# One-hot rows of the second key: the subtraction moved from ScalarE's biased Abs to one GpSimd instruction per four tokens

## The reference

```python
def chunk(xc):
    ...
    sc = jnp.einsum('chpd,hpkd->chpk', q, sub_keys)          # two sets of 128 sub keys per head
    sv, si = lax.top_k(sc, PEER_TOPK)
    ...
    idx = jnp.take_along_axis(cidx, fi, axis=-1)             # expert = 128 * first key + second key
    g = jax.nn.softmax(fv, axis=-1)
    u = u_tab[idx]
    a = jax.nn.gelu(jnp.einsum('chkd,cd->chk', u, xc))
    vv = v_tab[idx]
    return jnp.einsum('chk,chkd->cd', g * a, vv)
```

## Time and profile before

| | us |
|---|---|
| median of 3 runs | 2059.51 |
| lowest and highest of them | 2057.79, 2061.49 |
| the profiled execution's own time | 2063.19 |
| its span from first to last instruction | 2061.5 |
| PE busy | 1805.8 (88% of the span) |
| DVE busy | 1194.0 (58%) |
| ACT busy | 908.6 (44%) |
| POOL busy | 333.3 (16%) |

### The profile page before, as it was taken

How to read it: one execution, slowest core, us unless ns; L and a number is a source line. 1 busy time by engine, 2 the same in 40 slices (tenths; PEclk the granted TensorE clock), 3 DMA queues, 4 the chain that set the end, 5 groups by cost and what they waited for, 6 DMA issues and landing times.

```text
span 2061.5 us, 36645 instructions
## 1 busy us (share of the span) xinstructions
PE 1805.8 (88%) x11980; PEld 1636.2 (79%) x11980; DVE 1194.0 (58%) x2304; ACT 908.6 (44%) x1664; POOL 333.3 (16%) x206
## 2 busy tenths in 40 slices
PE   7999799998979887977878798889998659999997
PEld 6899578787979667965878688889997558888886
DVE  2685566665444454454542699984445985555554
ACT  2564431312334444433342233335446994555553
POOL 2000000000000000020000276668884000000000
PEclk9999999999989998988898899999999999999999
DMA  8755112121436203510452254456552016666553
GB/s 280 217 183 172 32 31 61 31 61 61 141 105 183 72 0 110 181 61 0 143 130 55 84 161 151 148 152 180 180 177 71 0 45 207 192 193 192 192 192 119
DMA packets 214867, 254.91 MB, mean 124 GB/s; under 512 B 14919, under 2 KB 196907, under 8 KB 214827
## 3 DMA queue, kind: packets, MB, share of 16 engines
q1 hardware_dynamic: 214827, 254.39, 40.5%
HBM read 253.29 MB, written 1.05 MB: 123 GB/s over the span
## 4 chain that ended last, share of the span: by engine, by line
PE 55%; issue 20%; DVE 8%; POOL 7%; ACT 4%; DMA 3%; SPq 1%; DVEq 1%; POOLq 0%; ACTq 0%; PEldq 0%
PE ps L1875 17%; PE ps L1520 15%; POOL w_lo L540 6%; PE ps L1833 3%; DVE raw L1460 3%; DMA raw<-in_u_experts 3%; PE ps L1688 2%; PE ps L1648 2%; PE ps L1647 2%; PE ps L1638 2%; DVE arena L1134 2%; PE ps L1562 1%; PE ps L1621 1%; DVE raw L1341 1%; SPq L446 1%
## 5 line engine op out<-in xcount | busy, mean ns | idle before, releaser
L540 POOL TENSOR_TENSOR w_lo<-raw,w_hi 128x1024 fp32r<-128x1024 f32 x128 | 307.3, 2406 | 345.3 <-ACT w_hi L878 344.3
L1520 PE MATMUL ps<-x_hi,w_hi 128*128 128x256 f32 x1104 | 323.1, 293 | 26.7 <-DVE w_lo L950 13.9
L1833 PE MATMUL ps<-x_hi,w_hi 128*128 128x256 f32 x1024 | 297.4, 290 | 33.8 <-ACT arena L883 26.3
L1520 PE MATMUL ps<-x_lo,w_hi 128*128 128x256 f32 x1104 | 320.8, 291 | 0.0
L1520 PE MATMUL ps<-x_hi,w_lo 128*128 128x256 f32 x1104 | 320.7, 290 | 0.0
L1833 PE MATMUL ps<-x_lo,w_hi 128*128 128x256 f32 x1024 | 294.6, 288 | 0.0
L1833 PE MATMUL ps<-x_hi,w_lo 128*128 128x256 f32 x1024 | 294.3, 287 | 0.0
L1520 PEld LDWEIGHTS ps<-x_hi,w_hi 128*128 128x128 f32 x1104 | 220.6, 200 | 30.4 <-issue 14.2
L1485 DVE TENSOR_TENSOR w_lo<-raw,w_hi 128x1024 fp32r<-128x1024 f32 x128 | 156.9, 1226 | 148.3 <-ACT w_hi L938 148.3
L878 ACT ACTIVATE w_hi<-raw 128x1024 fp32r<-128x1024 f32 x128 | 135.6, 1060 | 239.6 <-DVE raw L1341 239.6
L1833 PEld LDWEIGHTS ps<-x_hi,w_hi 128*128 128x128 f32 x1024 | 201.1, 196 | 37.8 <-ACT arena L883 23.3
(11 more groups left out here) (322 smaller groups left out, 3328.8 us busy)
## 6 DMA issues: line engine op xcount, KB each, us to landing
raw<-in_u_experts SPq DMA_DIRECT2D x512, 128.0 KB, 2.6
raw<-in_v_experts SPq DMA_DIRECT2D x128, 512.0 KB, 3.5
arena<-in_ada_w SPq DMA_DIRECT2D x14, 1024.0 KB, 5.3
raw<-in_a_w_in SPq DMA_DIRECT2D x12, 1024.0 KB, 5.5
arena<-in_a_w_in SPq DMA_DIRECT2D x12, 1024.0 KB, 5.4
raw<-in_b_w_in SPq DMA_DIRECT2D x8, 1024.0 KB, 5.6
arena<-in_b_w_in SPq DMA_DIRECT2D x8, 1024.0 KB, 5.6
raw<-in_w_in SPq DMA_DIRECT2D x8, 1024.0 KB, 5.4
```

Of the source, the lines that this page charges most:

```text
L540: pool.tensor_tensor(UTL[e], UT[e % 2], UTH[e].bitcast(F32), ALU.subtract).then_inc(utl_ready, 1)
L1520: ins = mm(o[:, b * S:b * S + S], w[:, slot, kk, b * P:b * P + P], xx[:, kk, :], start=(kk == 0 and n == 0), stop=(kk == k - 1 and n == 2))
L1833: ins = mm(ps[e % 2][:, 0:S], w[e % 4][:, kk * P:kk * P + P], xx[:, kk, :], start=(kk == 0 and n == 0), stop=(kk == KC - 1 and n == 2))
```

## The change

POOL gets the subtraction: for each group it waits for the free slot (`g_ps`), then adds `iota`, read four times over, and the columns of minus b of four tokens, each read 128 times over, and writes 4 x 128 columns into the slot of `OHJ` in one `tensor_tensor`. It counts a new semaphore, `ohj_diff`. ACT waits for that instead of `g_ps` and takes Abs of all 512 columns in one activation, in place, with no bias. `rows_j` is as it was. `distance` now counts on 512 columns, one instruction in place of four. The DMA of the convolution's weights is counted by `vec_in` too, and `conv_in` is gone; PE waits for 15 DMAs on `vec_in` instead of for 14 and one.

```diff
-        x_in, conv_in, vec_in, rows_in = sem("x_in"), sem("conv_in"), sem("vec_in"), sem("rows_in")
+        x_in, vec_in, rows_in = sem("x_in"), sem("vec_in"), sem("rows_in")
+        ohj_diff = sem("ohj_diff")
...
-            sp.dma_start(S1, a_conv_w.rearrange("a i (b p) -> (a i b) p", p=P)).then_inc(conv_in, 16)
+            sp.dma_start(S1, a_conv_w.rearrange("a i (b p) -> (a i b) p", p=P)).then_inc(vec_in, 16)
...
+            pool.wait_ge(hkt_ready, 2)
+            with pool.Fori(0, S // 16) as i:
+                for c in range(4):
+                    pool.wait_ge(g_ps, 4 * i + (c + 1))
+                    tok = HKT[:, 1, bass.ds(16 * i + 4 * c, 4)].unsqueeze(2).broadcast_to([P, 4, NK])
+                    pool.tensor_tensor(OHJ[:, c, :, :], iota.unsqueeze(1).broadcast_to([P, 4, NK]), tok, ALU.add).then_inc(ohj_diff, 1)
...
             def distance(c, i):
-                g = c % 4
-                act.wait_ge(g_ps, 4 * i + (c + 1))
-                for q in range(4):
-                    ins = act.activation(OHJ[:, g, q, :], iota, ACT.Abs, bias=HKT[:, 1, bass.ds(16 * i + (4 * c + q), 1)])
-                ins.then_inc(ohj_abs, 1)
+                act.wait_ge(ohj_diff, 4 * i + (c + 1))
+                act.activation(OHJ[:, c % 4, :, :], OHJ[:, c % 4, :, :], ACT.Abs).then_inc(ohj_abs, 1)
...
-            pe.wait_ge(conv_in, 16)
-            pe.wait_ge(vec_in, 16 * 14)
+            pe.wait_ge(vec_in, 16 * 15)
```

## The result

The changed kernel takes 2087.55 us (median of 4 runs, 2084.08 to 2088.48), the kernel before 2059.74 in the 4 runs beside it. The ratio is 1.0132 (95% interval 1.0115 to 1.0150): the change costs 27.8 us. The profiled execution took 2088.19, with a span of 2086.5.

The account below looks back on a forecast made before the run. ACT was taken to bound the one-hot stage, DVE close behind; 59 turns at 2.61 us and two groups at 1.70 after the start end it 51.4 us later: 2059.5 + 51.4 = 2111 us, range 2082 to 2134.

Parts of the forecast that it names:

- ACT's relief: One-hot stage: ACT sets the pace, DVE a close second; freeing ACT wins at most 0.06 to 0.15 us per group.
- free period of 1.70: One-hot stage: DVE's time per group when it waits for nobody, 1.70 us, taken from readings of 1.72 and 1.63.
- The rival of the other sign: Line 1460 not excluded by POOL, DVE runs free: stage gains 3.7 to 8 us, 2055 us in all; chance 0.12.
- The exclusion: POOL and DVE's tensor_scalar at line 1460 wait for each other's whole instruction; one held by POOL ends 0.09 us later.
- 285 + 65 = 350 against 342: Line 1460's duration, estimated at the fast rate against measured ns, read as showing it runs in the blocked ones' fast way.
- G: Duration of one POOL tensor_tensor of 512 columns: 1.20 us, with ends of 1.06 and 1.45.
- the rival of the slow POOL: POOL slow on repeated reads: 1.45 us per turn, period 2.9, 2128 us; chance 0.12 together with no overlap.
- The new period: One-hot stage: POOL arrives just ahead of each group's fourth tensor_scalar and holds it: 1.32 + 1.20 + 0.09 = 2.61 us.
- the first rival: POOL arrives after the fourth tensor_scalar and hides behind weigh: 2.23 to 2.4 us per group, 2089 us at 2.23; chance 0.18.
- The start: One-hot stage's first three groups: POOL takes four turns in a row from about 1576.9; third group's rows end at 1585.2.
- The sum: 1585.2 + 59 x 2.61 + 2 x 1.70 puts the last rows at 1742.6, last products at 1743.8: +51.4 us.
- my likeliest arrangement: One-hot stage: each POOL turn holds one group's fourth tensor_scalar, period 2.5 to 2.75 us; chance 0.58.

Follow-up runs that it names:

- e2_no_pool: Changed kernel without POOL's instruction, ACT taking Abs of whatever stands in the slot (rows not those of the reference): 2047.55 us, ratio 0.9938.
- e1_pool_beside: Kernel before, ACT's four biased Abs kept, plus POOL's 64 tensor_tensor of 512 columns into a spare tile nobody reads: 2086.24 us, ratio 1.0116.
- e7_psum_input: Changed kernel with line 1460 as scalar_tensor_tensor, 128 PSUM columns in place of the weight (weights left out): 2050.46 us in one run.
- e9_iota_in_psum: Changed kernel with line 1460's tensor_scalar reading iota from PSUM, not SBUF (version not complete): 2066.98 us, ratio 1.0032.
- e11_weight_in_psum: Changed kernel, whole computation kept, line 1460 as scalar_tensor_tensor with iota in SBUF and the weight's column read from PSUM: 2046.23 us, ratio 0.9924.
- e4_half_timed: Changed kernel with POOL's turn held until rows of group c-2 end and only two tokens per group; ACT does the others by biased Abs: 2056.41 us, ratio 0.9980.
- e5_pe_filler: Changed kernel with three more 128-column products of a zero tile per group on PE: 2081.63 us, ratio 1.0093.
- e3_timed: Changed kernel with one more wait on POOL, its turn for group c starting when rows of group c-2 have ended: 2085.80 us, ratio 1.0112.

## Why the prediction was right, and where its terms were off

- **What bounded before, and what ACT's relief is worth.** Right in kind: ACT was the bound, DVE a close second. `e2_no_pool` makes it 14 us (12.2 in the stage), where I had 4 to 8 without the exclusion. My free period of 1.70 was too careful; it is 1.63, and the period before was 1.80 ((1689.66 - 1579.87) / 61 from the earlier trace rows), not 1.76. The rival of the other sign didn't take place, and I had priced it too small.
- **The exclusion.** Right. It was read from three pairs of rows in another stage, and it is shown here by `e1_pool_beside`, where POOL's work is all that was added. By the Trainium skill ("SBUF — State Buffer", Who interferes with whom) a DVE instruction with at most one SBUF input, outside the modes that use two ports, does not contend with GpSimd. The trace agrees: the forms with one input in PSUM (`weigh`, `e7_psum_input`, `e9_iota_in_psum`, `e11_weight_in_psum`) were never held. That line 1460 is one of the held ones was right too, but the reading that I took it from, 285 + 65 = 350 against 342, is not borne out as a test: the form of `e7_psum_input` and `e11_weight_in_psum`, which POOL never holds, takes 329 to 333 ns, no more than the held one. The duration could not tell the two apart.
- **G.** Mis-sized: 1.20 forecast, 1.04 measured, just under my low end of 1.06. This add is cheaper per column than the subtract of the earlier trace rows that I scaled from: 613 ns for 256 columns in `e4_half_timed` and 1038 for 512 are 1.66 ns per column. Reading over and over costs POOL nothing that shows: those 256 columns take 613, the plain add of 255 took 608, so the rival of the slow POOL didn't take place. 59 x 0.16 = 9.4 us of the miss.
- **The new period.** This is the step that failed: "POOL arrives just ahead of the fourth, and the pattern repeats". At the full clock POOL arrives 1.39 us after a group's rows end, not 1.32, and the fourth `tensor_scalar` of a free group starts at about 1.29, not 1.38, since `weigh` starts 0.08 before the last row has ended. The order that I had decided by 0.06 us is the other way round by 0.10. What I had as the first rival, a turn that hides beside `weigh`, took place in 16 of 60 groups; the others paid for a turn or, where the products were slow, for parts of two. The mean is 2.21 us instead of the 2.45 that my formula gives with the measured G. 59 x 0.24 = 14 us. That the rival's time was 2089 us and 2087.6 was measured is luck: its period of 2.23 was 4 x 0.257 + 1.20. With the measured G the same sum gives 2.07, which is what `e5_pe_filler` shows at the full clock; the changed kernel lost the other 0.14 to the lower clock, for which I had no term.
- **The start.** 8.5 us forecast from the first row to the end of the third group, 6.97 measured, the shorter turns again.
- **The sum.** +51.4 forecast, +27.7 in the stage. The difference of 23.7 us is 22.3 in the 61 periods (157.4 forecast, 135.1 measured: the two terms above, less 1.0, since I had two of the groups at 1.70 and the mean of 2.21 counts them like the rest) and 1.5 at the start. The time lay inside the range, 23 us under my middle of 2111 and among the rivals' times rather than those of my likeliest arrangement (a period of 2.5 to 2.75).
- **PE's clock** had no term. I had every group of products at 1.13 us. The clock fell to 0.77 in the stage, 37 of the 61 groups of products from group 3 on took over 1.2 us, up to 2.08, and `e5_pe_filler` shows what follows: at the full level the changed kernel is 8 us faster, since the turns then alternate regularly. Whether the lower level costs anything by itself, apart from scattering the turns, was not tried.
- **Not costed and rightly so:** the DMA counted on another semaphore; the third phase, which starts when the last product ends and is as long as before.

## What to carry to other kernels

Before moving work to an idle GpSimd, look at what VectorE does at that time: a turn costs VectorE what of it overlaps instructions of the excluded forms, whoever needs the result. Where VectorE's instruction took its second tensor from PSUM, the two ran side by side; where it can't, a turn should be short enough to fit beside one that does. The length of an instruction doesn't tell whether it is of an excluded form. And where the order of two engines is decided by less than 0.1 us, forecast both orders and don't call one of them the likeliest.

## What the hardware showed that I had not expected

- `scalar_tensor_tensor` with the second tensor in PSUM (one column read 128 times over, by a register's offset) and one column operand takes 329 ns at 128 columns, with starts 0.26 us apart, no more than the `tensor_scalar` with two column operands (334 to 342). With the first input in PSUM the `tensor_scalar` takes 398, with starts 0.32 apart.
- A `tensor_scalar` held by POOL from before its start ends 0.08 us after POOL's end, and POOL held by one starts 0.07 to 0.15 late: the exclusion itself is passed on at almost no cost.
- The granted clock of the stage differed between versions of the same work: 1.00 with 1.13 to 1.16 us of products every 1.6 to 1.8 us (`e11_weight_in_psum`, before), 0.84 with a group every 2.14 us (`e3_timed`), 0.77 with one every 2.2 us on average, 1.00 again with 0.83 us of fillers per group (`e5_pe_filler`).
